# Prompt attention of a hybrid decoder step: scores between the two heads' transpositions, products with v one unit later

## The reference, cut to what matters

```python
def nsa_attend(q, q_pos, k_cmp, v_cmp, ks_blk, vs_blk, kw, vw, kw_pos, gates, table):
    ...
    s_s = jnp.einsum('btgrd,btgkd->btgrk', q, k_sel) * SCALE + t5_bias(table, dist_s)
    p_s = masked_softmax(s_s, mask_s[..., None, :])
    o_s = jnp.einsum('btgrk,btgkd->btgrd', p_s, v_sel)
    ...
    s_w = jnp.einsum('btgrd,bkgd->btgrk', q, kw) * SCALE
    s_w = s_w + t5_bias(table, jnp.broadcast_to(dist_w[:, None, :], (tq, G_KV, kw.shape[1])))[None]
    p_w = masked_softmax(s_w, mask_w[None, :, None, None, :])
    o_w = jnp.einsum('btgrk,bkgd->btgrd', p_w, vw)
    return gates[..., 0:1] * o_c + gates[..., 1:2] * o_s + gates[..., 2:3] * o_w
```

## Time and profile before

| | us |
|---|---|
| median of 3 runs | 2168.15 (2166.66 to 2174.38) |
| the profiled execution | 2165.16 |
| its span | 2163.5 |
| TensorE busy in it | 2119.7 |

### The profile page before, as it was taken

How to read it: one execution, slowest core, us unless ns; L and a number is a source line. 1 busy time by engine, 2 the same in 40 slices (tenths; PEclk the granted TensorE clock), 3 DMA queues, 4 the chain that set the end, 5 groups by cost and what they waited for, 6 DMA issues and landing times.

```text
span 2163.5 us, 48812 instructions
## 1 busy us (share of the span) xinstructions
PE 2119.7 (98%) x21488; PEld 1870.2 (86%) x21488; DVE 1061.7 (49%) x1780; ACT 412.1 (19%) x1181; POOL 505.4 (23%) x377
## 2 busy tenths in 40 slices
PE   8999999999999999999999999999999999999997
PEld 8999977777777779999999999777777877799996
DVE  3564344443726523773655543444437165237745
ACT  1111112222103411110111121222221043111002
POOL 3343300002011114334323343000020112134331
PEclk9999999999999999999999999999999999999999
DMA  7544332335542365444344443332264434544541
GB/s 277 184 167 157 127 138 101 101 100 210 205 137 98 114 224 189 158 169 173 127 166 170 161 157 127 119 101 101 101 217 169 137 118 144 207 171 162 174 173 65
DMA packets 88979, 329.50 MB, mean 152 GB/s; under 512 B 11904, under 2 KB 11920, under 8 KB 86464
## 3 DMA queue, kind: packets, MB, share of 16 engines
q1 hardware_dynamic: 74592, 268.60, 35.7%
q0 software_dynamic: 11872, 53.59, 7.0%
q10 hardware_dynamic: 2304, 4.20, 0.6%
HBM read 315.91 MB, written 18.82 MB: 155 GB/s over the span
## 4 chain that ended last, share of the span: by engine, by line
PE 88%; DVE 7%; DMA 3%; issue 1%; ACT 0%; POOL 0%; SPq 0%; DVEq 0%; POOLq 0%
PE PB L783 24%; PE PB L833 3%; PE PB L851 3%; PE PB L847 3%; PE PB L837 3%; PE PB L842 3%; PE PB L824 3%; PE PB L827 3%; PE PB L1239 3%; DMA WT<-in_w_all 2%; PE PB L808 1%; PE PB L907 1%; PE PB L989 1%; PE PB L972 1%; PE PB L974 1%; PE PB L967 1%
## 5 line engine op out<-in xcount | busy, mean ns | idle before, releaser
L783 PE MATMUL PB<-XT,WT 128*128 128x264 f32 (+1 forms) x2816 | 692.7, 395 | 1.6 <-DMA WT<-in_w_all 1.5
L783 PEld LDWEIGHTS PB<-XT,WT 128*128 128x128 f32 (+1 forms) x2816 | 508.8, 189 | 103.4 <-issue 15.2
L1438 ACT ACTIVATE VT<-PB 128x132 f32<-128x132 f32 (+2 forms) x280 | 79.1, 291 | 581.3 <-PE PB L837 132.6
L1438 ACT ACTIVATE ARENA<-PB 128x128 f32<-128x128 f32 (+6 forms) x185 | 75.5, 430 | 233.7 <-PE PB L1089 62.2
L618 POOL DMA_DIRECT2D out<-in_c_win x16 | 8.1, 506 | 457.2 <-DVE ARENA L2005 457.2
L618 POOL DMA_DIRECT2D ARENA<-in_c_sel x64 | 40.0, 625 | 230.3 <-issue 230.3
L639 POOL TENSOR_TENSOR TOEP<-WT 128x1024 f32<-128x1024 f32 x20 | 47.2, 2358 | 186.0 <-PE PB L837 133.8
L639 POOL TENSOR_TENSOR TOEP<-H 128x1024 f32<-128x1024 f32 x20 | 48.2, 2408 | 138.3 <-PE PB L837 133.9
L833 PE MATMUL PB<-ARENA,TOEP 128*128 128x132 f32 x640 | 78.6, 276 | 1.7 <-POOL TOEP L642 1.7
L837 PE MATMUL PB<-ARENA,TOEP 128*128 128x132 f32 x640 | 78.5, 276 | 0.0
L842 PE MATMUL PB<-ARENA,TOEP 128*128 128x132 f32 x640 | 78.5, 276 | 0.0
(11 more groups left out here) (456 smaller groups left out, 4134.3 us busy)
## 6 DMA issues: line engine op xcount, KB each, us to landing
WT<-in_w_all SPq DMA_DIRECT2D x340, 512.0 KB, 4.5
H<-in_w_all SPq DMA_DIRECT2D x120, 512.0 KB, 4.6
KNVC<-in_w_all SPq DMA_DIRECT2D x40, 512.0 KB, 4.2
out<-in_c_win POOLq DMA_DIRECT2D x16, 512.0 KB, 5.1
ARENA<-in_c_cmp POOLq DMA_DIRECT2D x64, 128.0 KB, 5.2
ARENA<-in_c_sel POOLq DMA_DIRECT2D x64, 128.0 KB, 4.0
TOEP<-in_toep POOLq DMA_DIRECT2D x2, 2048.0 KB, 9.2
ARENA<-in_states POOLq DMA_DIRECT2D x4, 1024.0 KB, 11.2
```

The costliest lines, as they stand in the source:

```text
L783: ins = mm(PB[rows, bank, 0:T], WT[:, s, k, 0:rows.stop - rows.start], x, start=start, stop=stop)
L1438: return act(out, in_, ACT.Copy)
```

## The change

- Scores of unit u+2 are issued between the transpositions of head 0 and of head 1 of unit u; before, they stood ahead of both.
- The products with v of unit u-1 are issued after head 1's transpositions of unit u, from one of two `PTS` buffers in turn. The second lies in `KNVC`. They have a step list of their own, `po_t`.
- VectorE copies the result of unit u-2, one unit later than before; ScalarE's copy of head 0 waits for the products with v of unit u-2.
- The tables: 5 products per unit (1 behind the scores, 4 after the products with v) instead of 7; in the last two units 3 stand behind head 0's transpositions. `cb` gets 12 instead of 8, `vec` 101 instead of 98, `as2` 6 instead of 4. By `plan()` the attention up to the end of `pt1` of the last unit holds 63 products in place of 69, and `gates` 123 in place of 122.

```diff
-BEHIND_MIX = {..., "vec": 98, ...
+BEHIND_MIX = {..., "vec": 101, ...
-BEHIND_MIX.update({"cb": 8, "cbt": 3, "sc1": 4})
+BEHIND_MIX.update({"cb": 12, "cbt": 3, "sc1": 4})
...
-    BEHIND_MIX.update({f"pt0{unit}": 3, f"pt1{unit}": 3, f"o{unit}": 0})
+    BEHIND_MIX.update({f"pt0{unit}": 0, f"pt1{unit}": 4, f"o{unit}": 0})
+BEHIND_MIX[f"pt0{UNITS - 2}"] = BEHIND_MIX[f"pt0{UNITS - 1}"] = 3
...
-BEHIND_MIX.update({"as0": 12, "as1": 36, "as2": 4, "as3": 3})
+BEHIND_MIX.update({"as0": 12, "as1": 36, "as2": 6, "as3": 3})
...
-        PTS, PCT, VCP = take(P, 2, 2, 3 * P), take(P, NG, SEQ), take(P, 4 * HD)
+        PTS = [take(P, 2, 2, 3 * P), KNVC[:, 8 * HD:8 * HD + 12 * P].rearrange("p (e b n) -> p e b n", e=2, b=2)]
+        PCT, VCP = take(P, NG, SEQ), take(P, 4 * HD)
...
+                for u in range(UNITS):
+                    it = L * UNITS + u
+                    pe.wait_ge(*step("pv_v", it, "ps"))
+                    if u:
+                        pe.wait_ge(*step("pv_a", it - 1, "pt1"))
+                    else:
+                        pe.wait_ge(*step("cb_a", L, "pt"))
+                    transposed(u, 0)
+                    if u + 2 < UNITS:
+                        pe.wait_ge(*step("sc_v", it + 1, "add"))
+                        scores(u + 2)
+                        project(L, f"sc{u + 2}")
+                    else:
+                        project(L, f"pt0{u}")
+                    pe.wait_ge(*step("pv_a", it, "pt0"))
+                    transposed(u, 1)
+                    if u:
+                        weighted(u - 1)
+                    project(L, f"pt1{u}")
+                weighted(UNITS - 1)
+                project(L, f"o{UNITS - 1}")
...
-                    if u + 2 < UNITS:
-                        take_out(L, f"sc{u + 2}")
                     for e in range(2):
+                        if e and u + 2 < UNITS:
+                            take_out(L, f"sc{u + 2}")
                         sc.wait_ge(*step("pv_t", it, f"pt{e}"))
-                        if e == 0 and u:
-                            sc.wait_ge(*step("pv_t", it - 1, "o"))
-                        mark("pv_a", it, copy(PTS[:, e], PB[:, 3:5, 0:3 * P]), f"pt{e}")
+                        if e == 0 and u > 1:
+                            sc.wait_ge(*step("po_t", it - 2, "o"))
+                        mark("pv_a", it, copy(PTS[u % 2][:, e], PB[:, 3:5, 0:3 * P]), f"pt{e}")
...
-                    if u:
-                        taken(u - 1)
+                    if u > 1:
+                        taken(u - 2)
+                taken(UNITS - 2)
                 taken(UNITS - 1)
```

More of the change, by code:

```diff
@@ L103 @@
     BEHIND.update({f"r{chunk}": 1, f"u{chunk}": 1, f"s{chunk}": chunk // (NCH - 1)})
-BEHIND_MIX = {"v0": 4, "v1": 4, "v2": 4, "v3": 4, "vec": 98, "mu": 5, "mu2": 3, "sq": 0, "var": 10, "gbc": 5, "bc2": 5,
+BEHIND_MIX = {"v0": 4, "v1": 4, "v2": 4, "v3": 4, "vec": 101, "mu": 5, "mu2": 3, "sq": 0, "var": 10, "gbc": 5, "bc2": 5,
               "h0": 12, "out0": 46, "h1": 12, "out1": 10}
-BEHIND_MIX.update({"cb": 8, "cbt": 3, "sc1": 4})
+BEHIND_MIX.update({"cb": 12, "cbt": 3, "sc1": 4})
 for unit in range(UNITS):
@@ L381, in hybrid_trunk @@
         steps("sc", DEPTH * UNITS, t="s0 s1 s", v="add max", a="exp")
-        steps("pv", DEPTH * UNITS, t="pt0 pt1 o", v="rc cg ps", a="pt0 pt1")
-        steps("po", DEPTH * UNITS, v="o")
+        steps("pv", DEPTH * UNITS, t="pt0 pt1", v="rc cg ps", a="pt0 pt1")
+        steps("po", DEPTH * UNITS, v="o", t="o")
         steps("as", DEPTH, t="sc0 sc1 pt n o tr", a="exp pt os", v="zero q gm gsr add max rc cg ps back")
@@ L1299, in _, with transposed, weighted @@
                 project(L, "sc1")
-                for u in range(UNITS):
+                def transposed(u, e):
+                    it = L * UNITS + u
+                    s0, s1 = SS[u % 3]
+                    for br in range(2):
+                        transpose(PB[:, 3 + br, 0:P], s0[:, 2 * e + br, :])
+                        for q in range(2):
+                            ins = transpose(PB[:, 3 + br, P + q * P:2 * P + q * P], s1[:, 2 * e + br, q * P:q * P + P])
+                    mark("pv_t", it, ins, f"pt{e}")
+                def weighted(u):
                     it = L * UNITS + u
                     g2, r = divmod(u, 4)
-                    if u + 2 < UNITS:
[L1304 to L1321, removed]
                     pe.wait_ge(*step("pv_a", it, "pt1"))
@@ L1325, in _ @@
                     col = (u % 2) * 256
+                    pts = PTS[u % 2]
                     for br in range(2):
@@ L1330, in _ @@
                                 if t == 0:
-                                    mm(PB[half(e), 5, col:col + 256], v, PTS[:, e, br, 0:SEQ], start=br == 0, stop=False)
+                                    mm(PB[half(e), 5, col:col + 256], v, pts[:, e, br, 0:SEQ], start=br == 0, stop=False)
                                 else:
-                                    mm(PB[half(e), 5, col + P:col + 256], v, PTS[:, e, br, SEQ:3 * P], start=False, stop=False)
+                                    mm(PB[half(e), 5, col + P:col + 256], v, pts[:, e, br, SEQ:3 * P], start=False, stop=False)
                     rows = slice(32 * r, 32 * r + NBLK)
@@ L1337, in _ @@
                         ins = mm(PB[half(e), 5, col:col + 256], VCP[rows, g * HD:g * HD + HD], PCT[rows, g, :], start=False, stop=True)
-                    mark("pv_t", it, ins, "o")
-                    project(L, f"o{u}")
+                    mark("po_t", it, ins, "o")
+                for u in range(UNITS):
+                    it = L * UNITS + u
+                    pe.wait_ge(*step("pv_v", it, "ps"))
[17 more added lines that the diff above has]
+                project(L, f"o{UNITS - 1}")
                 before(pe, "po_v", (L + 1) * UNITS)
@@ L2167, in taken @@
                     it = L * UNITS + u
-                    ve.wait_ge(*step("pv_t", it, "o"))
+                    ve.wait_ge(*step("po_t", it, "o"))
                     mark("po_v", it, cp(H[:, Q0 + u, 0:SEQ], PB[:, 5, (u % 2) * 256:(u % 2) * 256 + 256]), "o")
```

## The result

The changed kernel takes 2186.76 us (median, 2181.14 to 2191.55), the kernel before beside it 2167.40: a ratio of 1.0086, 95% interval 1.0067 to 1.0106, about 19 us slower. 2187 was forecast, in a range of 2175 to 2199. The profiled execution of the changed kernel is the slowest shown, 2191.55 us with a span of 2189.6, so lengths of steps are read from it and the total from the median.

The account below looks back on a forecast made before the run. TensorE was taken to bound the kernel, busy 2119.7 of 2163.5 us. Added 14.2 us without the clock and 6.0 of clock give 2185.4 from 2165.16, or 2188.4 by the median; forecast 2187, range 2175 to 2199.

Parts of the forecast that it names:

- The loop: In each unit, scores to scaled probabilities (7.53 us) plus head 0's transpositions (0.65): no unit shorter than 8.18 us.
- TensorE's own unit: TensorE's work per unit in attention is 7.16 us, so it waits 1.02 us in each unit.
- Four products in `cb` cover nothing: They delay unit 1's scores by 1.79 us; at unit 0 TensorE waits 4.02 us where it waited 1.81.
- Unit 1: Ahead of unit 1's transpositions TensorE waits 3.05 us, having no products with v of an earlier unit to do.
- ScalarE at unit 6: With only 3 products between at unit 6, ScalarE leaves TensorE waiting 0.3 to 0.7 us once, taken as 0.5.
- The clock: Behind the long waits at units 0 and 1, four falls in all at 1.5 us each: +6.0 us.
- The rival in which short waits bring falls: Ten waits of 1.02 us in the units cost 1.5 us each, 15 us more: 2202 us; chance 0.13.
- The sum: Attention 7.0 and 5.5 us longer, products elsewhere 1.05 and 0.6: 14.2 us without the clock, 20.2 in total.
- What the change was to win: Waits near the edits, 7.3 us over both layers: 3.6 at unit 0, 2.0 behind `vec`, 1.7 behind `as2`.

Follow-up runs that it names:

- after_no_max: The changed kernel with VectorE's two row maxima of each unit replaced by one small memset of the bias; 2173.23 us, ratio 1.0031.
- cb_back: The changed kernel with 4 products moved from `cb` (12 to 8) to `sc1` (4 to 8), behind the scores of unit 1; 2184.98 us, ratio 1.0098.
- with all waits filled: The changed kernel with `cb` 8, `sc1` 13, 10 products behind unit 0 and 6 behind each of units 1 to 5; 2169.42 us, ratio 1.0026.
- with the long waits filled: The changed kernel with `cb` 8, `sc1` 13 and 10 products behind unit 0, units 1 to 5 keeping 4; 2167.19 us, ratio 1.0012.
- v_same_unit: The changed kernel with the products with v back in their own unit, behind the 4 products; 2180.77 us, ratio 1.0062.
- the filled old order: The kernel before with 4 more products behind unit 2's scores, `vec` 101 and `as2` 6, taken from `gates`; 2154.11 us, ratio 0.9955.

## Why the prediction was right, and where its terms were off

**The loop** was the step on which it stood, and it is shown three ways: opened by moving the scores (2163), shortened by taking work off VectorE (8.41 to 7.45 us a unit with TensorE's list unchanged), and kept while the late products with v were undone (2181). The chain from scores to probabilities was put at 7.53 us and measured 7.53 and 7.60. The loop was put at 8.18 and is 8.41, mostly because scores behind transpositions start 0.81 us after them and not 0.65. I took the 0.65 from transpositions ahead of ordinary products; ahead of scores they take 0.75 without a wait (711.88 to 712.63 in the run without the maxima) and 0.81 behind one, and that pair stood nowhere in the old order. That is 0.23 us in each of 12 units, 2.8 us too little.

**TensorE's own unit** was put at 7.16 us from the earlier trace rows and is 7.45, seen in the units of after_no_max without a wait. Counted by starts TensorE had 8.41 - 7.45 = 0.96 us to spare in a unit, for the 1.02 forecast; the trace calls 0.74 of it idle, since it models the ends of matmuls. As the loop sets the time, the error costs nothing.

**Four products in `cb` cover nothing.** The wait at unit 0 is 3.99 and 4.00 us where 4.02 was forecast. Against the run cb_back, the shift of unit 1's scores by 1.8 us is plain in the trace; that it makes the whole kernel slower is not shown by the total.

**Unit 1** was to wait 3.05 us and waited 1.90 and 2.06, because unit 0's work ran at the lower clock in that time and so ended later.

**ScalarE at unit 6** waited 0.83 us in each layer for the 0.5 forecast, for the reason given.

**The clock.** I charged four falls at 1.5 us. Behind the waits for VectorE there was one in each layer, at the 4.0 us wait, and it reached past unit 0's transpositions: these took 1.47 us for 0.81, and from the scores behind them to the next scores it was 701.60 - 691.88 = 9.72 us, where the steady loop takes 8.41. That is 2.0 us a layer, 3.9 in both for my 6.0. The rule of the Trainium skill (TensorE: Matmul & The Clock Gate, "HAM oscillation — how this bites in real kernels"), a cold start behind every long enough gap, agrees with the trace at 4.0 us in both layers. Shorter waits show both outcomes, so at 1.8 us the one row that agreed with it could not decide. The clock fell behind 1.82 us in the second layer of the kernel before, behind 1.82 and 1.81 with all waits filled, behind 1.79 and 2.27 in both layers without the maxima, and behind 2.21 and 2.89 us in the first layer of cb_back; it stayed up behind 1.81 us in the first layer of the kernel before, behind 1.90 and 2.06 us here, and behind 2.21 and 2.89 us in the second layer of cb_back. The row that I cited for the first layer in the earlier trace rows covers the wait alone; over 686 to 694 us, behind it, the clock was 1.00 too. The rival in which short waits bring falls did not happen: with the long waits filled, twelve waits of up to 0.74 us stood in a stage with a granted clock of 1.00 and 0.99, and in v_same_unit the five waits of 0.93 and 0.94 us of the first layer in one with 1.00 (694 to 736 us). No run has waits of the full 1.02 us in every unit.

**The sum.** Attention grew by 11.3 us in each layer, 22.6, where 7.0 and 5.5 without the clock were forecast. The 10.1 between them is, rounded, 3.9 of clock (6.0 forecast), 2.8 of the loop, 0.7 of ScalarE at unit 6 (2 x 0.83 less the 1.0 forecast), 1.5 of a fall of the clock behind the scores of `cb` in the second layer, and 1.3 in the last two units. There it is 759.37 - 742.83 = 16.54 us from unit 6 to the end where 15.54 was forecast; 0.33 of that is ScalarE's wait, and the rest are steps read too short, such as 0.65 for transpositions that take 0.75 ahead of products with v. 3.3 us more of the profiled span lie ahead of `vec` (530.39 before, 533.72 after), where nothing was changed. So the profiled execution is 26.4 us above the one before, and the medians 19.4 apart: the forecast of 2187 met the median closer than its terms deserve. That is luck in the number: a term too high (the clock) and terms too low (the loop, ScalarE and the end) cancel in part, and the account above is of one execution of each kernel, the changed one's slowest. Which of its terms are smaller in the median execution is not shown.

**What the change was to win** was there: 2.0 us behind `vec` and 1.7 behind `as2` went. With the wait at unit 0 and its fall of the clock the filled old order is worth 10.5 us in the medians (2154 against 2165), where the waits and the fall come to 8.8; the other 1.7 are not accounted for. None of it needed the new order.

## What to carry to other kernels

Before moving a step behind a wait, ask whether what releases that wait comes out of the step itself one round earlier. If so, the round can't be shorter than that chain plus the step, and its length can be read beforehand from any place where the engine already waited for the same chain. Filler pays only between the start of a chain and the wait for its end; ahead of the start it moves both. And an engine's list carries waits across: a tile that ended late held back exponentials, and these the copy that was wanted.

## What the runs showed of the hardware

TensorE's clock also fell with no wait at all. In the changed kernel it was 0.79 over 1757 to 1765 us with TensorE busy for 8.00 of 8.00 us, behind the 64 matmuls of 15 columns of `cb`; the twelve products there took 6.24 us, 0.52 each. From the first matmul of `cb` to the scores of unit 1 it was 14.45 us, where the second layer of the kernel before took 11.21 and the four products more are 1.79, so the fall cost 1.5 us. The kernel before had one at this place in its first layer (0.79 over 668 to 676) and none in its second. Why is open.
